# A two-layer decoder trunk on one core: the input also loaded with features on partitions, and a new order of the first loads and products

## The chip, the cores and the metric

The kernel runs on one NeuronCore of a Trainium2 chip. The metric is the device time of one execution in microseconds (us); lower is better. The engines are TensorE (PE in the profile; its weight loads are PEld), VectorE (DVE), ScalarE (ACT), GpSimd (POOL) and SyncE (SP), which here only issues DMAs.

## What is computed

The input `x` is 256 tokens of 1024 features in float32. Each of two layers computes, in the reference:

```
h = _rms_norm(x, attn_norm[layer])
x = x + _hybrid_mixer(h, w_in[layer], ...)
h = _rms_norm(x, ffn_norm[layer])
x = x + _swiglu(h, w_ffn_up[layer], w_ffn_down[layer])
```

with `_rms_norm(x, gain) = x * rsqrt(mean(x*x) + 1e-6) * gain`. The mixer begins with `proj = h @ w_in`, and goes on with four token mixers, gates, and the branch and output products. Only the very first of these products, `h @ w_in` of layer 0 with its norm, is touched by the change.

## The kernel before, in words

**Products in three parts.** Every float32 matrix is split in a high and a low part (`w_hi`, `w_lo`; `hT_hi`, `hT_lo`), rounded to TensorE's fp32r type. A product is three matmuls: high by high, high by low weight, low by high weight. ScalarE makes the high parts by a copy (L718 for weights, L722 for the left side), VectorE the low parts by subtraction (L977, L984).

**Units.** All weights go through the core once. They are cut into 144 units a layer; a unit is two blocks of 128 rows (`k`) by 512 columns, 512 KB. SP loads a unit into `raw` (six slots), ScalarE and VectorE split it into `w_hi` and `w_lo` (five slots), TensorE multiplies it with two token tiles `t` of 128 tokens: 2 k x 2 t x 3 parts = 12 matmuls of 512 columns. The first four units are the eight k blocks of the item `dq` of the first combined projection. ScalarE and VectorE work `AHEAD = 4` units ahead of TensorE; between units each engine takes other stages from a timetable by unit number, which the change leaves as it is.

**The norm.** The per-token factor of the norm is applied to products afterwards. The left side is `x * gain`, turned so that features lie on partitions: `hT[part][:, k, t*128:(t+1)*128]`. The squares for the factor are summed by `row_squares` (L734) on ScalarE.

**The first unit before.** SP issues the loads in written order: a half of a token tile of `x`, unit 0, a half tile, unit 1, two half tiles, units 2 to 5. ScalarE's queue loads the identity matrix and the norm's gains. TensorE runs 24 warm-up matmuls (L1674), turns the gains (L1680), turns `x` tile by tile with the identity (`turn_x`, L1655), with more warm-ups between, and VectorE multiplies the turned banks by the gain (`first_gain`, L1319). ScalarE and VectorE split the result, and TensorE starts the products of unit 0 (`first_products`, L1667). The unit 3 is the first that goes through the common routine `multiply` (L1636, L1637, L1640).

Signals are counting semaphores: `hi_ready` and `lo_ready` count split units, `unit_done` the units that TensorE has finished, `lhs_hi` and `lhs_lo` the parts of the left side.

Of the kernel before, what the change touches and what calls it, by code (L numbers as in the profile page):

```python
# [110 lines left out]
RING = 5  # L111
AHEAD = 4
# [196 lines left out]
def build(nc, x, attn_norm, ffn_norm, w_in, b_gate, w_branch, w_out, w_ffn_up, w_ffn_down, consts, params, out):  # L309
# [8 lines left out]
    with ExitStack() as ctx:  # L318
        def sb(name, shape, dt=F32, stack=ctx, align=32):
            return stack.enter_context(nc.sbuf_tensor(name, shape, dt, align_bytes=align))  # L320

        event_order = {}


        first_turn = {(*kind, t, b): 2 * b + t + 1 for kind in (("tr_norm", "attn"), ("norm", "attn"))
                      for t in range(TT) for b in range(2)}

        def signal(name, events):

            events = list(events)  # L330
            semaphore = ctx.enter_context(nc.semaphore(name))
            event_order[id(semaphore)] = {e: i + 1 for i, e in enumerate(events)}
            assert len(event_order[id(semaphore)]) == len(events)
            return semaphore

        def nth(semaphore, layer, event):

            order_in_layer = event_order[id(semaphore)]
            if layer == 0 and event in first_turn:
                return first_turn[event]  # L340
            return layer * len(order_in_layer) + order_in_layer[event]
# [27 lines left out]
        gain_rows = sb("gain_rows", [KD, P])  # L369
        gain_column = sb("gain_column", [P, KD])  # L370
# [56 lines left out]

        def hn(t):
            return wide[:, t, 0:D]
# [33 lines left out]
        stage_done = signal("stage_done", STAGE_EVENTS)  # L463
        lhs_hi = signal("lhs_hi", evac_events(ACT_ORDER))
        lhs_lo = signal("lhs_lo", evac_events(DVE_ORDER))
        warm_ready, bands_loaded = sem("warm_ready"), sem("bands_loaded")
        identity_loaded, consts_loaded, params_loaded = sem("identity_loaded"), sem("consts_loaded"), sem("params_loaded")
        x_loaded = [[sem(f"x_loaded{t}{j}") for j in range(2)] for t in range(TT)]
        gain_rows_loaded, gain_rows_turned = sem("gain_rows_loaded"), sem("gain_rows_turned")
        gain_column_ready = sem("gain_column_ready")  # L470
# [44 lines left out]
        hn_ready = {w: signal(f"hn_ready_{w}", [(t, j) for t in range(TT) for j in range(2)]) for w in ("attn", "ffn")}  # L515
# [26 lines left out]
        def _(sp):  # L542
# [21 lines left out]
            def load_x(t, j):  # L564
# [799 lines left out]
        def _(pe):  # L1364
# [324 lines left out]
            for t in range(TT):  # L1689
                turn_x(t, 1)  # L1690
# [81 lines left out]
```

## Time and profile before

| what | value |
| --- | --- |
| median of 3 runs | 866.67 us (866.63 to 866.77) |
| profiled execution, its own time | 866.5 us |
| its span, first to last instruction | 864.7 us |
| TensorE busy | 860.1 us (99% of the span), 4247 matmuls |
| VectorE busy | 599.4 us (69%) |
| ScalarE busy | 441.4 us (51%) |
| GpSimd busy | 110.1 us (13%) |
| DMA | 159.48 MB, mean 184 GB/s |

The span and the device time of the same execution differ by 1.8 us, which lies outside the first and last instruction. Busy times of different engines overlap. A matmul's own duration is its way through the array; the next one starts sooner, so the pace is read from the distance of starts. A group of n equal instructions in the timeline has one start and one length, from the first start to the last end.

### The profile page before, as it was taken

How to read it: one execution, taken by the hardware profiler on the slowest of the kernel's cores; microseconds unless marked ns; L12 is line 12 of the kernel's file. 1: busy time of each engine (PE TensorE's matmuls, PEld its weight loads, DVE VectorE, ACT ScalarE, POOL GpSimd, SP SyncE). 2: the span in 40 equal slices, each digit the busy share in tenths (PEclk: the TensorE clock that was granted, in tenths of full speed). 3: DMA queues.
4: the chain of work that ended last, by engine and by line, in shares of the span. 5: the costliest groups of instructions: out<-in, count | busy, mean ns of one | idle time of the engine just before them, and what ended most of it. 6: DMA issues, size and time to landing. Idle time of an engine off the chain costs nothing.

```text
span 864.7 us, 11127 instructions
## 1 busy us (share of the span) xinstructions
PE 860.1 (99%) x4247; PEld 712.1 (82%) x4247; DVE 599.4 (69%) x847; ACT 441.4 (51%) x639; POOL 110.1 (13%) x89
## 2 busy tenths in 40 slices
PE   9999999999999999999999999999999999999998
PEld 7888888888888888888888888888888888888886
DVE  5996887768777556654479868777597765565542
ACT  6556564754454444443375574556543644444431
POOL 0740100004501000000005401000064000000000
PEclk9999999999999999999999999999999999999999
DMA  9656565575657666555665455655666476665541
GB/s 331 201 185 179 173 189 171 161 236 183 207 171 237 192 178 190 192 175 193 171 184 166 130 183 168 194 176 175 210 195 193 127 238 177 190 185 181 194 146 50
DMA packets 87366, 159.48 MB, mean 184 GB/s; under 512 B 7432, under 2 KB 13712, under 8 KB 87312
## 3 DMA queue, kind: packets, MB, share of 16 engines
q1 hardware_dynamic: 87152, 158.69, 59.1%
q8 instruction: 34, 0.56, 0.2%
q14 instruction: 20, 0.16, 0.1%
q10 hardware_dynamic: 160, 0.07, 0.0%
HBM read 157.69 MB, written 1.05 MB: 184 GB/s over the span
## 4 chain that ended last, share of the span: by engine, by line
PE 99%; DMA 0%; DVE 0%; issue 0%
PE bulk L1636 30%; PE bulk L1640 30%; PE bulk L1637 30%; PE bankAB L1386 2%; PE bulk L1667 1%; PE bankAB L1577 1%; PE bankT L1530 0%; PE bankAB L1519 0%; DMA con<-consts_dram 0%; PE bankAB L1477 0%; PE bankAB L1395 0%; PE bankO L1490 0%; PE bankO L1548 0%; PE bankO L1577 0%; PE bankT L1577 0%; PE bankO L1395 0%
## 5 line engine op out<-in xcount | busy, mean ns | idle before, releaser
L977 DVE TENSOR_TENSOR w_lo<-raw,w_hi 128x1024 fp32r<-128x1024 f32 (+1 forms) x288 | 361.6, 1268 | 162.4 <-ACT w_hi L718 159.8
L718 ACT ACTIVATE w_hi<-raw 128x1024 fp32r<-128x1024 f32 (+1 forms) x288 | 299.0, 1048 | 237.5 <-PE bulk L1640 233.7
L1636 PE MATMUL bulk<-w_hi,hT_hi 128*128 128x512 f32 (+1 forms) x884 | 346.5, 392 | 0.0
L1637 PE MATMUL bulk<-w_lo,hT_hi 128*128 128x512 f32 (+1 forms) x884 | 340.8, 386 | 0.0
L1640 PE MATMUL bulk<-w_hi,hT_lo 128*128 128x512 f32 (+1 forms) x884 | 338.1, 386 | 0.0
L1640 PEld LDWEIGHTS bulk<-w_hi,hT_lo 128*128 128x128 f32 x884 | 165.7, 188 | 33.8
L1636 PEld LDWEIGHTS bulk<-w_hi,hT_hi 128*128 128x128 f32 x884 | 166.1, 188 | 33.3 <-issue 1.6
L1637 PEld LDWEIGHTS bulk<-w_lo,hT_hi 128*128 128x128 f32 x884 | 166.2, 188 | 31.4
L1636 PE MATMUL bulk<-w_hi,aT_hi 128*128 128x512 f32 x176 | 68.8, 391 | 0.0
L1640 PE MATMUL bulk<-w_hi,aT_lo 128*128 128x512 f32 x176 | 68.5, 389 | 0.0
L1637 PE MATMUL bulk<-w_lo,aT_hi 128*128 128x512 f32 x176 | 68.5, 389 | 0.0
L690 POOL TENSOR_TENSOR wide<-wide 128x512 f32<-128x512 f32 x24 | 46.1, 1943 | 125.2 <-DVE wide L1262 124.8
L656 POOL TENSOR_TENSOR wide<-wide,ropeA 128x512 f32<-128x512 f32 x8 | 12.0, 1494 | 210.9 <-DVE wide L1069 210.9
L1640 PEld LDWEIGHTS bulk<-w_hi,aT_lo 128*128 128x128 f32 x176 | 33.0, 188 | 7.0
L1637 PEld LDWEIGHTS bulk<-w_lo,aT_hi 128*128 128x128 f32 x176 | 33.0, 188 | 6.8
L1636 PEld LDWEIGHTS bulk<-w_hi,aT_hi 128*128 128x128 f32 x176 | 33.0, 188 | 6.7
L1636 PE MATMUL bulk<-w_hi,oT_hi 128*128 128x512 f32 x80 | 31.3, 391 | 0.0
L1640 PE MATMUL bulk<-w_hi,oT_lo 128*128 128x512 f32 x80 | 31.1, 389 | 0.0
L1637 PE MATMUL bulk<-w_lo,oT_hi 128*128 128x512 f32 x80 | 31.1, 389 | 0.0
L914 ACT ACTIVATE wide<-bulk,y_ffn 128x512 f32<-128x512 f32 (+1 forms) x24 | 14.4, 651 | 18.2 <-PE bulk L1640 16.0
L1252 DVE SCALAR_TENSOR_TENSOR wide<-bulk,y_attn,bias 128x512 f32<-128x512 f32 x32 | 22.5, 744 | 1.4 <-PE bulk L1640 1.4
L1276 DVE SCALAR_TENSOR_TENSOR wide<-bulk,y_ffn,wide 128x512 f32<-128x512 f32 (+1 forms) x24 | 15.9, 702 | 10.2 <-ACT wide L914 10.2
(259 smaller groups left out, 711.7 us busy)
## 6 DMA issues: line engine op xcount, KB each, us to landing
raw<-in_w_in_dram SPq DMA_DIRECT2D x112, 512.0 KB, 4.4
raw<-in_w_ffn_up_dram SPq DMA_DIRECT2D x80, 512.0 KB, 4.4
raw<-in_w_ffn_down_dram SPq DMA_DIRECT2D x44, 512.0 KB, 3.3
raw<-in_w_branch_dram SPq DMA_DIRECT2D x20, 512.0 KB, 4.1
raw<-in_w_out_dram SPq DMA_DIRECT2D x16, 512.0 KB, 3.3
bias<-in_b_gate_dram SPq DMA_DIRECT2D x16, 256.0 KB, 4.9
raw<-in_w_ffn_up_dram SPq DMA_DIRECT2D x16, 256.0 KB, 3.4
raw<-in_w_in_dram SPq DMA_DIRECT2D x8, 256.0 KB, 2.6
```

Of the source, the lines that this page charges most:

```text
L656: pool.tensor_tensor(ta, x, ropeA[:, i, t:t + 1, :].broadcast_to([P, 8, HD]), ALU.mult)
L690: ins = pool.tensor_tensor(m, m, wide[:, t, n * D + j * NC:n * D + (j + 1) * NC], ALU.add)
L718: act.activation(w_hi[:, g % RING, :, 0:width], raw[:, g % RAW, :, 0:width], ACT.Copy).then_inc(hi_ready, 1)
L914: act.activation(ff_tmp(t, p, width), item_bank(layer, ITEM_AT[item], t)[:, 0:width], ACT.Sigmoid, scale=y_ffn[:, t:t + 1]).then_inc(ff_si ...
L977: vec.tensor_tensor(w_lo[:, g % RING, :, 0:width], raw[:, g % RAW, :, 0:width], w_hi[:, g % RING, :, 0:width].bitcast(F32), ALU.subtract). ...
L1252: vec.scalar_tensor_tensor(out=wide[:, t, g * NC:(g + 1) * NC], in0=item_bank(layer, ITEM_AT[("gate", g)], t), scalar=y_attn[:, t:t + 1], ...
L1276: vec.scalar_tensor_tensor(out=s, in0=item_bank(layer, ITEM_AT[item], t)[:, 0:width], scalar=y_ffn[:, t:t + 1], in1=s, op0=ALU.mult, op1=A ...
L1386: ins = pe.matmul(dst, a[a_part], b[b_part], start=start and a_part + b_part == 0, stop=stop and a_part == 1, skip_group_check=True)
L1577: ins = pe.transpose(bank[name][:, k * P:(k + 1) * P], ff_act(t, p, blocks * P)[:, k * P:(k + 1) * P], identity)
L1636: pe.matmul(dst, hi, whi, start=(k == ks[0]), stop=False)
L1637: pe.matmul(dst, hi, wlo, start=False, stop=False)
L1640: ins = pe.matmul(dst, lo, whi, start=False, stop=(k == ks[-1]))
```

## The change

The host makes one more input, `turned_x`: the eight gain columns and `x` transposed, 128 partitions by 8 + 8 x 256 columns of float32, 1 MB. The plain `x` is still loaded, for the residual and the squares. The transposes of `x` and of the gains, the products with the gain on VectorE out of PSUM, the separate load of the identity and the load of the gains are gone. The gain is applied as the per-partition scale of ScalarE's copy and of VectorE's subtraction.

```diff
+WARM = 34
+FIRST_SQUARES = [1, 2]
...
+            def load_turned_x(e):
+                c0 = KD + e * 2 * SEQ
+                part = slice(c0 if e else 0, c0 + 2 * SEQ)
+                sp.dma_start(wide[:, 0, part], turned_x[:, part]).then_inc(turned_x_loaded[e], 16)
+            def load_x(t):
+                sp.dma_start(x_sb[:, t, :], x[0, t * P:(t + 1) * P, :]).then_inc(x_loaded[t], 16)
-            load_x(0, 0)
-            load_unit(0)
-            load_x(1, 0)
-            load_unit(1)
-            load_x(0, 1)
-            load_x(1, 1)
-            for g in range(2, RAW):
+            load_turned_x(0)
+            sp.dma_start(raw[:, 0, 1, :], w_in[0, P:2 * P, OFF["dq"]:OFF["dq"] + NC]).then_inc(raw_loaded[0], 16)
+            for g in range(1, 4):
+                load_turned_x(g)
                 load_unit(g)
+            load_x(0)
+            load_unit(4)
+            load_x(1)
+            load_unit(5)
...
+            def first_hi(k):
+                act.wait_ge(turned_x_loaded[k // 2], 16)
+                act.activation(hT[0][:, k, :], first_x[:, k, :], ACT.Copy, scale=first_gain[:, k:k + 1]).then_inc(lhs_hi, 1)
+            act.dma_start(raw[:, 0, 0, :], w_in[0, 0:P, OFF["dq"]:OFF["dq"] + NC]).then_inc(first_tile_loaded, 16)
+            act.preload_act_table_set("natural_log_exp_and_others")
+            first_hi(0)
+            first_hi(1)
+            act.wait_ge(first_tile_loaded, 16)
+            act.activation(w_hi[:, 0, 0, :], raw[:, 0, 0, :], ACT.Copy).then_inc(first_tile_ready, 1)
+            act.wait_ge(raw_loaded[0], loaded[0])
+            act.activation(w_hi[:, 0, 1, :], raw[:, 0, 1, :], ACT.Copy).then_inc(hi_ready, 1)
             for g in range(1, AHEAD):
+                first_hi(2 * g)
+                first_hi(2 * g + 1)
                 split_hi(g)
             for g in range(DEPTH * U):
+                if g in FIRST_SQUARES:
+                    row_squares(0, "attn", FIRST_SQUARES.index(g))
...
+            def first_lo(k):
+                vec.wait_ge(lhs_hi, k + 1)
+                vec.scalar_tensor_tensor(out=hT[1][:, k, :], in0=first_x[:, k, :], scalar=first_gain[:, k:k + 1],
+                                         in1=hT[0][:, k, :].bitcast(F32), op0=ALU.mult, op1=ALU.subtract).then_inc(lhs_lo, 1)
+            for g in range(AHEAD):
+                first_lo(2 * g)
+                first_lo(2 * g + 1)
                 split_lo(g)
...
+            def first_unit(u):
+                tiles = range(2 * u, 2 * u + 2)
+                for k in tiles:
+                    pe.wait_ge(lhs_hi, k + 1)
+                    if k == 0:
+                        pe.wait_ge(first_tile_ready, 1)
+                    else:
+                        pe.wait_ge(hi_ready, nth(hi_ready, 0, u))
+                    for t in range(TT):
+                        pe.matmul(item_bank(0, 0, t), hT[0][:, k, t * P:(t + 1) * P], w_hi[:, u, k % 2, :], start=(k == 0), stop=False)
+                for k in tiles:
+                    pe.wait_ge(lhs_lo, k + 1)
...
+                pe.wait_ge(lo_ready, nth(lo_ready, 0, u))
...
-            warm_up(24)
...
+            warm_up(WARM)
+            for u in range(KD // 2):
+                first_unit(u)
```

On TensorE the program's beginning before is this (`warm` is the warm-up operand, `con` holds the identity, `hT` is the left side):

```order
L1674 MATMUL bulk<-warm 128x128 x24
L1680 MATMUL bankO<-con,gain_rows 128x8
L1655 MATMUL bankAB<-con,x_sb 128x128 x4
L1674 MATMUL bulk<-warm 128x128 x8
L1655 MATMUL bankT<-con,x_sb 128x128 x4
L1674 MATMUL bulk<-warm 128x128 x6
L1667 MATMUL bulk<-w_hi,hT_hi 128x512 x2
L1667 MATMUL bulk<-w_hi,hT_lo 128x512 x2
L1667 MATMUL bulk<-w_hi,hT_hi 128x512 x2
L1655 MATMUL bankAB<-con,x_sb 128x128 x4
L1655 MATMUL bankO<-con,x_sb 128x128 x4
L1667 MATMUL bulk<-w_lo,hT_hi 128x512 x4
```

And this of the changed kernel, with the first two units:

```order
L1671 MATMUL bulk<-warm 128x128 x34
L1653 MATMUL bulk<-w_hi,hT_hi 128x512 x4
L1657 MATMUL bulk<-w_hi,hT_lo 128x512 x4
L1662 MATMUL bulk<-w_lo,hT_hi 128x512 x4
L1653 MATMUL bulk<-w_hi,hT_hi 128x512 x4
L1657 MATMUL bulk<-w_hi,hT_lo 128x512 x4
L1662 MATMUL bulk<-w_lo,hT_hi 128x512 x4
```

The 17 turning matmuls are gone, the warm-ups stand in one block of 34 instead of 24, 8 and 6, and every early unit is 4 + 4 + 4 products.

On SP, which issues the loads, the beginning before:

```order
L567 DMA x_sb<-in_x_dram 128x512
L556 DMA raw<-in_w_in_dram 128x2x512
L567 DMA x_sb<-in_x_dram 128x512
L556 DMA raw<-in_w_in_dram 128x2x512
L567 DMA x_sb<-in_x_dram 128x512 x2
L556 DMA raw<-in_w_in_dram 128x2x512 x6
L605 DMA con<-consts_dram 128x1028
```

and of the changed kernel (`wide` is a work area that holds the turned input at first):

```order
L571 DMA wide<-turned_x_dram 128x520
L578 DMA raw<-in_w_in_dram 128x512
L571 DMA wide<-turned_x_dram 128x512
L559 DMA raw<-in_w_in_dram 128x2x512
L571 DMA wide<-turned_x_dram 128x512
L559 DMA raw<-in_w_in_dram 128x2x512
L571 DMA wide<-turned_x_dram 128x512
L559 DMA raw<-in_w_in_dram 128x2x512
L575 DMA x_sb<-in_x_dram 128x1024
L559 DMA raw<-in_w_in_dram 128x2x512
L575 DMA x_sb<-in_x_dram 128x1024
L559 DMA raw<-in_w_in_dram 128x2x512 x3
```

A quarter of the turned input now stands ahead of each of the first four units, the token rows stand behind unit 3, and the first half of unit 0 has moved to ScalarE's queue.

ScalarE of the changed kernel begins so:

```order
L951 DMA raw<-in_w_in_dram 128x512
L952 ACT_TABLE_LOAD
L949 ACTIVATE hT_hi<-wide 128x256 x2
L956 ACTIVATE w_hi<-raw 128x512
L959 ACTIVATE w_hi<-raw 128x512
L949 ACTIVATE hT_hi<-wide 128x256 x2
L728 ACTIVATE w_hi<-raw 128x1024
L949 ACTIVATE hT_hi<-wide 128x256 x2
L728 ACTIVATE w_hi<-raw 128x1024
L949 ACTIVATE hT_hi<-wide 128x256 x2
L728 ACTIVATE w_hi<-raw 128x1024 x2
L744 ACTIVATE wide,ssq<-x_sb 128x512 x2
```

Unit 0 is split in two copies, the first of which TensorE can already use; the squares (L744) stand behind the split of unit 4, where before they stood behind that of unit 3.

## Rows read from the trace of the kernel before

**Rows 1.** Page, part 4: the chain that ended last, by engine.
```profile
PE 99%; DMA 0%; DVE 0%; issue 0%
```

**Rows 2.** Timeline of PE from 0 us: start, us, engine, line, instruction.
```profile
0.97 2.74 PE L1674 MATMUL bulk<-warm 128*128 128x128 bf16 x24 [0.97 <-DVE warm L1311]
4.15 0.27 PE L1680 MATMUL bankO<-con,gain_rows 8*128 8x8 f32 x1 [0.43 <-DMA con<-consts_dram]
6.34 1.11 PE L1655 MATMUL bankT<-con,x_sb 128*128 128x128 f32 x4
16.66 1.08 PE L1667 MATMUL bulk<-w_lo,hT_hi 128*128 128x512 f32 x4
17.58 0.39 PE L1636 MATMUL bulk<-w_hi,hT_hi 128*128 128x512 f32 x1
20.32 0.39 PE L1636 MATMUL bulk<-w_hi,hT_hi 128*128 128x512 f32 x1
```

**Rows 3.** Timeline of PE, narrow windows around the first products, one instruction each.
```profile
7.85 0.78 PE L1667 MATMUL bulk<-w_hi,hT_hi 128*128 128x512 f32 x1
8.43 0.55 PE L1667 MATMUL bulk<-w_hi,hT_hi 128*128 128x512 f32 x1
8.84 0.50 PE L1667 MATMUL bulk<-w_hi,hT_lo 128*128 128x512 f32 x1
9.17 0.39 PE L1667 MATMUL bulk<-w_hi,hT_lo 128*128 128x512 f32 x1
```

**Rows 4.** Window 4.2 to 8.9: engines' busy us, then PEclk, DMA share, GB/s.
```profile
4.20:8.90 4.70, 4.67 (x26) 3.76 (x26) 2.27 (x5) 2.31 (x4) 0.00 (x0) 1.00 1.01 354
```

**Rows 5.** Timeline of ACT and DVE: a whole unit, and 256-column operations.
```profile
5.31 1.06 ACT L718 ACTIVATE w_hi<-raw 128x1024 fp32r<-128x1024 f32 x1 [2.23 <-DMA raw<-in_w_in_dram]
8.70 1.22 DVE L977 TENSOR_TENSOR w_lo<-raw,w_hi 128x1024 fp32r<-128x1024 f32 x1
...
34.74 0.38 ACT L812 ACTIVATE keys_hi<-bankT 128x256 fp32r<-128x256 f32 x1 [0.51 <-PE bankT L1423]
35.02 0.38 ACT L813 ACTIVATE keys_hi<-bankT 128x256 fp32r<-128x256 f32 x1
...
43.24 0.41 DVE L1174 TENSOR_TENSOR keys_lo<-bankT,keys_hi 128x256 fp32r<-128x256 f32 x1
```

**Rows 6.** Timeline of SP's queue: start and us of the first issues.
```profile
0.72 0.38 SPq L567 DMA_DIRECT2D x_sb<-in_x_dram  x1
1.16 0.42 SPq L556 DMA_DIRECT2D raw<-in_w_in_dram  x1
1.63 0.46 SPq L567 DMA_DIRECT2D x_sb<-in_x_dram  x1
2.13 0.43 SPq L556 DMA_DIRECT2D raw<-in_w_in_dram  x1
3.60 8.46 SPq L556 DMA_DIRECT2D raw<-in_w_in_dram  x6
```

**Rows 7.** DMAs issued at 0.72, 1.16, 1.63, 2.13, 3.60: us to landing last.
```profile
x_sb<-in_x_dram SPq DMA_DIRECT2D x1, 256.0 KB, 3.2
raw<-in_w_in_dram SPq DMA_DIRECT2D x1, 512.0 KB, 4.1
x_sb<-in_x_dram SPq DMA_DIRECT2D x1, 256.0 KB, 4.7
raw<-in_w_in_dram SPq DMA_DIRECT2D x1, 512.0 KB, 6.1
raw<-in_w_in_dram SPq DMA_DIRECT2D x1, 512.0 KB, 7.3
```

**Rows 8.** Timeline, ACT and POOL later in layer 0, with their waits.
```profile
26.02 1.06 ACT L718 ACTIVATE w_hi<-raw 128x1024 fp32r<-128x1024 f32 x1 [1.24 <-PE bulk L1640]
...
22.19 1.50 POOL L641 TENSOR_TENSOR ropeA<-con,parameters 128x128 f32<-128x128 f32 x1 [20.92 <-DMA parameters<-params_dram]
30.66 1.29 POOL L656 TENSOR_TENSOR wide<-wide,ropeA 128x512 f32<-128x512 f32 x1 [4.06 <-DVE wide L1069]
```

More of the change, by code:

```diff
@@ L306, in constant_blocks, with build @@
     return {n: np.ascontiguousarray(b, dtype=np.float32) for n, b in blocks.items()}
-def build(nc, x, attn_norm, ffn_norm, w_in, b_gate, w_branch, w_out, w_ffn_up, w_ffn_down, consts, params, out):
+def build(nc, x, attn_norm, ffn_norm, w_in, b_gate, w_branch, w_out, w_ffn_up, w_ffn_down, consts, params, turned_x, out):
     cblocks = constant_blocks()
@@ L320, in sb, with signal @@
             return stack.enter_context(nc.sbuf_tensor(name, shape, dt, align_bytes=align))
[L322 to L328, printed above, removed]
+        event_order, more_in_first = {}, {}
+        first_norm = {("norm", "attn", t, b): 4 * (b + 1) for t in range(TT) for b in range(2)}
+        def signal(name, events, more=0):
             events = list(events)
@@ L1644, in multiply @@
                     ins.then_inc(early_done, 1)
-            def turn_x(t, b):
-                name = "ABTO"[2 * t + b]
-                pe.wait_ge(x_loaded[t][b], 16)
-                if name == "O":
-                    pe.wait_ge(gain_column_ready, 1)
-                take(name, lhs_lo, 0, ("norm", "attn", t, b))
-                for k in range(4):
-                    ins = pe.transpose(bank[name][:, k * P:(k + 1) * P], x_sb[:, t, (4 * b + k) * P:(4 * b + k + 1) * P], identity)
-                ins.then_inc(stage_done, 1)
@@ L1658, in first_products @@
-            def first_products(u, t, a_part, b_part):
-                event = ("norm", "attn", t, (2 * u) // 4)
-                dst = item_bank(0, 0, t)
-                if a_part:
-                    wait_low(0, event)
-                else:
-                    wait_high(0, event)
-                for k in range(2 * u, 2 * u + 2):
-                    ins = pe.matmul(dst, hT[a_part][:, k, t * P:(t + 1) * P], (w_hi, w_lo)[b_part][:, u, k % 2, :],
-                                    start=(k == 0 and a_part + b_part == 0), stop=(k == KD - 1 and b_part == 1))
-                return ins
+            def first_unit(u):
[10 more added lines that the diff above has]
+                    pe.wait_ge(lhs_lo, k + 1)
+                    for t in range(TT):
+                        pe.matmul(item_bank(0, 0, t), hT[1][:, k, t * P:(t + 1) * P], w_hi[:, u, k % 2, :], start=False, stop=False)
+                pe.wait_ge(lo_ready, nth(lo_ready, 0, u))
+                last = u == KD // 2 - 1
+                for t in range(TT):
+                    for k in tiles:
+                        ins = pe.matmul(item_bank(0, 0, t), hT[0][:, k, t * P:(t + 1) * P], w_lo[:, u, k % 2, :], start=False,
+                                        stop=k == KD - 1)
+                    if last and t == 0:
+                        ins.then_inc(early_done, 1)
+                ins.then_inc(unit_done, 1)
```

110 lines of the change are left out of this document (27 added, 83 removed).

## The prediction

> **What bounds the kernel.** I read the chain that ended last first: 99% of it is TensorE [rows 1]. Then the timeline of TensorE: after its first matmul at 0.97 us it stands idle for data once, 0.43 us at 4.15, and never again [rows 2]. So the time is the time at which the weight stream gets going, plus a fixed amount of matmul work. I fix a milestone that both kernels have: the first matmul of unit 4, which is behind 48 products (4 units of 12). Before, unit 3 begins at 17.58 and unit 4 at 20.32, that is 2.74 us for 12 products, **0.228 us a product** [rows 2]. The first product starts at 7.85 [rows 3]. All that is behind unit 4 is the same list of matmuls in both kernels, so a shift of this milestone is a shift of the end, if nothing later comes too late.
>
> Two things lie in those first 20.32 us besides the products at their pace. First, 48 products at 0.228 are 10.94 us; from 7.85 to 20.32 there are 12.47. The other 1.5 us are turning of x (eight of the turning matmuls lie between products), and products at a slower pace. Second, that slower pace: the first four starts are 7.85, 8.43, 8.84 and 9.17, distances of 0.58, 0.41 and 0.33 us, not 0.228 [rows 3]. The 24 warm-ups of 128 columns take 2.74 us, 0.114 each [rows 2], and four times that is 0.456 for 512 columns, twice 0.228. TensorE thus works at about half its pace (1.2 instead of 2.4 GHz) until 8.9 us. The granted-clock column says 1.00 for 4.2 to 8.9 us [rows 4], which the distances contradict; I go by the distances. The Trainium skill ("TensorE: Matmul & The Clock Gate", the caveats of Part 1) warns that the recorded clock events of trn2 have been seen to be unreliable; the trace agrees with the warning. If the column were right, no early product would be slow, which is rival A's sum below.
>
> **When the first product can start after the change.** It needs a quarter of the turned x, the first half of unit 0, and three copies on ScalarE. The two loads are 260 and 256 KB on two queues, both issued at about 0.72, as the first load of x was. Landings before are issue plus the time to landing [rows 6, 7]: the first 256 KB at 3.9, unit 0 at 5.3 (with 64 KB of identity that makes 832 KB), the second 256 KB at 6.3 (1088), unit 1 at 8.2 (1600), unit 2 at 10.9 (2624, with the two other halves of x). If 516 KB landed as the first 256 did, 3.9 us is the lower bound; unit 0's 5.3 is the upper one. In between by bytes: 3.92 + (516 - 320)/512 x 1.34 = 4.4 us. I take 4.4, as the two queues share the engines. The Trainium skill ("DMA: Bandwidth & Descriptors", queues, rings and completion order) says that each DMA engine takes turns between queues, packet by packet; by that neither of the two loads is done early, and the lower bound of 3.9 is out. No row shows two large first loads on two queues.
>
> Then ScalarE: two copies of 256 columns follow each other in 0.28 us (34.74, 35.02), and a whole unit of 1024 takes 1.06 [rows 5]; half of that with a fixed part is about 0.63. So 4.4 + 0.05 + 0.28 + 0.28 + 0.63 + 0.05 = **5.7 us** for the first product, against 7.85. Bounds: 5.2 with the early landing, 6.5 with the late one.
>
> **What follows it.** Second half of unit 0: it lands by 772 KB at about 5.1, is copied by 6.3, and TensorE needs it after two slow products, at 6.6. VectorE's low parts of x take 0.41 each [rows 5] and are ready at about 5.6 and 6.0. Its low part of unit 0 takes 1.22 from 6.3, ready at 7.5, needed after eight products, at 5.7 + 8 x 0.43 = 9.1. Unit 1 with its turned x is complete at 1540 KB: 6.33 + 452/512 x 1.9 = 8.0 us, split high at 9.1. TensorE ends unit 0 at about 9.9, so 0.8 us of cover; if this cover is gone, each us costs a us. Unit 2 (2308 KB) lands at 10.0, is ready at 11.1, needed at 12.6. Unit 3 (3076 KB) at the 393 GB/s between units 1 and 2 lands at 12.1, ready at 13.1, needed at 15.3. ScalarE spends 0.28 + 0.28 + 1.06 = 1.6 us a unit and VectorE 0.41 + 0.41 + 1.22 = 2.0, both under TensorE's 2.74.
>
> **Sum.** 48 products at 0.228: 10.94. Slow ones: from 5.7 to 8.9 with 0.41 to 0.456 a product, about 0.43: 7.4 products, each 0.2 too long, 1.5 us. Milestone at 5.7 + 10.94 + 1.5 = 18.1; I add 0.1 for handovers between parts: 18.2 against 20.32, a gain of **2.1 us**. The start itself hardly matters: an earlier or later start by 1 us moves the milestone by only 0.55, since more or fewer slow products fit before 8.9.
>
> **What costs nothing, and its cover.** The turned input is 1 MB more, some 2.6 us of DMA at 393 GB/s, all ahead of unit 4. Unit 4 comes at 4100 KB, 14.7 us, ready at 15.8 and needed at 18.2; unit 5 at 5124 KB, 17.4, ready 18.5, needed 20.9. That is 2.4 us of cover. From then on the loads run faster than the 2.74 us a unit in which TensorE eats them (1.3 us a unit at 393 GB/s). The issues behind the new ones on SP's queue (0.45 us each, [rows 6]) are eight more by unit 5, instead of six; the landings by bytes are later than the issues, so they do not count. The consts and parameters queue behind these: parameters, which before arrived for GpSimd at 22.19, come some 1.3 us later, and GpSimd's table work behind them (4.4 us to 26.6) then ends at 27.9; VectorE's result, for which GpSimd waited 4.06 us until 30.66, comes at 28.6 now [rows 8]. Cover 0.7 us, and behind it the turned queries aren't needed for five more units. The squares of x (four, 1.3 us for two by the 0.63 a copy) move behind unit 4's and 5's splits, where ScalarE waits on TensorE anyway: it did so for 1.24 us at 26.02 [rows 8]. One table load of ScalarE is gone; ScalarE is ahead there, so it gives nothing. VectorE's four products with the gain were on the way to the first split and are in the start above.
>
> **Rivals.** (B is the forecast above.)
>
> A. *The pace is full from the first products on.* For: 34 warm-ups in one block, up to about 4.7 us, where before there were 24 up to 3.7. Against: before, four more stretches of work followed and the pace rose only at 8.9. Then unit 0 ends at 8.5 and unit 1 waits for its split at 9.1: 9.1 + 36 x 0.228 = 17.3, gain 3.0, **863.7 us**.
>
> C. *The pace rises later than 8.9.* Before, TensorE worked without a gap from 4.15 on and rose 4.75 us later. After the change there is a gap of a us before 5.7; 4.75 behind it is 10.4: 11 slow products, 5.7 + 10.94 + 2.2 + 0.1 = 18.9, gain 1.4, 865.3. With a rise at 12.3 it is 15.4 products, 19.8, gain 0.5, 866.2. The Trainium skill ("TensorE: Matmul & The Clock Gate", Part 1) lets an idle array fall back to half clock, which speaks for this one; no row before shows how a gap of 1 us works here. I take **865.5 us** for it.
>
> D. *Slower, by the same mechanism.* Each slow product costs 0.2, so the gain is gone with (20.32 - 16.7)/0.2 = 18 slow products, a rise at 13.5 us, and the kernel is slower by over 1.7 us with 27 of them, a rise at 17.2. If all 48 stay slow the milestone is at 26.3 and the time 6 us longer, **872 us**. Waits for loads would have to break the stream again and again for that; the covers above speak against it.
>
> E. *It changes nothing*, as some later stage is short of its data and sets the milestone back. Unit 5 would have to land at 21.8 instead of 17.4. Against: TensorE had no such wait at all [rows 1, 2]. **866.7 us**.
>
> **Numbers.** The profiled execution took 866.5 us, and the median of the runs is 866.67, so the difference is made there: 866.67 - 2.1 = **864.6 us**. Chances: B 0.45, A 0.25, C 0.20, D 0.06, E 0.04. 0.2% of the time, 1.7 us, is about what a measurement tells from no change. B lies between 864.3 and 865.1 by the bounds of the start (5.2 to 6.5), and counts as faster 9 times in 10, A always, C 1 in 5: 0.25 + 0.40 + 0.04 = 0.69. D is slower 2 in 3 times, 0.04, and 0.27 is left for the same. The range takes in A's 863.7 with some room for a first load that is early, and C down to a gain of 0.6: 863.4 to 866.1.
>
> **What would show it.** In the changed profile: first product at 5.7 us (5.2 to 6.5); the distances of the starts at 0.41 to 0.46 until about 8.9 and 0.228 after; the 37th product (unit 3) at 15.4, the first of unit 4 at 18.2; no idle TensorE after the first product; unit 4's first to last matmul of the kernel as long as before. A wait before unit 1 at about 8.5 means rival A. Slow distances beyond 10 us mean C or D. I am wrong as a whole if TensorE waits for a load behind unit 4, or if the first product isn't earlier than 6.9.

## The result and the profile after

| what | before | after |
| --- | --- | --- |
| median of 15 runs each | 866.61 us (866.25 to 866.97) | 868.62 us (867.18 to 868.92) |
| profiled execution, its span | 866.5, 864.7 us | 868.86, 867.1 us |
| TensorE busy | 860.1 us | 857.8 us |

The ratio of after to before is 1.0018, 95% interval 1.0011 to 1.0024: slower by some 0.2%, where 864.6 us was forecast. The runs of after lie at two levels, seven at 867.18 to 867.31 us and eight at 868.62 to 868.92; both are above every run of before, and the 1.5 us between them is part of what has to be explained.

The timeline of TensorE after the change, the same places as [rows 2] and then the first wait that the old kernel did not have:

```profile
0.97 3.81 PE L1671 MATMUL bulk<-warm 128*128 128x128 bf16 x34 [0.97 <-DVE warm L1326]
6.33 1.23 PE L1653 MATMUL bulk<-w_hi,hT_hi 128*128 128x512 f32 x4 [1.55 <-ACT w_hi L956]
7.40 1.09 PE L1657 MATMUL bulk<-w_hi,hT_lo 128*128 128x512 f32 x4
...
16.53 1.07 PE L1662 MATMUL bulk<-w_lo,hT_hi 128*128 128x512 f32 x4
17.43 0.39 PE L1632 MATMUL bulk<-w_hi,hT_hi 128*128 128x512 f32 x1
...
28.09 0.39 PE L1636 MATMUL bulk<-w_hi,hT_lo 128*128 128x512 f32 x1
32.08 0.47 PE L1632 MATMUL bulk<-w_hi,hT_hi 128*128 128x512 f32 x1 [3.60 <-DVE wide L1084]
```

The first product starts at 6.33 and unit 4 at 17.43 instead of 20.32: **2.89 us are won**. Then the last product of unit 7 starts at 28.09, and the first of unit 8 at 32.08, after 3.60 us in which TensorE stands. Before, the same two products are here:

```profile
30.98 0.39 PE L1640 MATMUL bulk<-w_hi,hT_lo 128*128 128x512 f32 x1
31.26 0.47 PE L1636 MATMUL bulk<-w_hi,hT_hi 128*128 128x512 f32 x1
```

Unit 8 starts 0.28 us behind its predecessor, and the timeline prints no wait. That is not slack: the PSUM bank (the memory in which TensorE adds up its products) that it needs came free just then, as VectorE's timeline of before shows (start, us, line), with unit 8's low part first, then the norm of `dq`, whose last operation reads the bank:

```profile
23.87 1.23 DVE L977 TENSOR_TENSOR w_lo<-raw,w_hi 128x1024 fp32r<-128x1024 f32 x1 [0.50 <-ACT w_hi L718]
25.01 0.28 DVE L1010 TENSOR_TENSOR stat<-ssq 128x2 f32<-128x2 f32 x1
...
29.82 1.29 DVE L1069 TENSOR_TENSOR wide<-bulk,stat 128x512 f32<-128x512 f32 x2
```

29.82 + 1.29 is 31.11, and TensorE, which would have been ready at 31.21 (30.98 + 0.23), starts at 31.26. Item `dk` (units 8 to 11) takes over the PSUM bank of item `dq` (units 0 to 3), and `multiply` makes TensorE wait for both token tiles' release by VectorE. After the change the same three rows, and ScalarE's high part of unit 8 ahead of them:

```profile
23.59 1.06 ACT L728 ACTIVATE w_hi<-raw 128x1024 fp32r<-128x1024 f32 x1 [1.58 <-DMA raw<-in_w_in_dram]
```
```profile
24.69 1.23 DVE L992 TENSOR_TENSOR w_lo<-raw,w_hi 128x1024 fp32r<-128x1024 f32 x1 [2.19 <-ACT w_hi L728]
25.83 0.42 DVE L1025 TENSOR_TENSOR stat<-ssq 128x2 f32<-128x2 f32 x1
...
30.65 1.29 DVE L1084 TENSOR_TENSOR wide<-bulk,stat 128x512 f32<-128x512 f32 x2
```

All is 0.8 us later, not 2.9 us earlier. VectorE stands 2.19 us for ScalarE, which stands 1.58 us for unit 8's load. The load explains only that part: had it been there, ScalarE would have begun unit 8 at 22.0, behind the work that it does with one idle stretch of 0.23 us from 14.35 on (the splits of units 4 to 7, four squares of `x`, two of `dq`), where before it began it at 22.78. So the 2.9 us were not there for VectorE in any case, but some 0.8. The DMA rows of unit 8 (issued before at 16.21, after at 12.23; the last number is us to landing), then of the first two loads after:

```profile
raw<-in_w_in_dram SPq DMA_DIRECT2D x1, 512.0 KB, 4.8
```
```profile
raw<-in_w_in_dram SPq DMA_DIRECT2D x1, 512.0 KB, 11.3
...
wide<-turned_x_dram SPq DMA_DIRECT2D x1, 260.0 KB, 4.0
raw<-in_w_in_dram ACTq DMA_DIRECT2D x1, 256.0 KB, 4.2
```

Unit 8 lands at 21.0 before and at 23.55 after. It is issued 4 us earlier, but stands behind 1 MB more, which is some 2.6 us at the prediction's 393 GB/s.

Behind the wait the pace is halved for a while. Windows of TensorE after: us, busy (matmul starts), granted clock, DMA share, GB/s.

```profile
31.00:32.00 1.00, 0.00 (x0) 1.00 0.05 20
32.00:33.00 1.00, 0.92 (x4) 0.85 0.00 0
33.00:36.00 3.00, 3.00 (x9) 0.50 0.11 18
36.00:40.00 4.00, 4.00 (x23) 0.99 0.80 245
```

A granted clock of 0.50 is the 1.2 GHz level. About 8 products start 0.43 instead of 0.23 us after each other, 1.6 us. **The whole sum**: -2.89 at unit 4, +3.71 between units 7 and 8 (from 28.09 to 32.08 is 3.99, before 0.28), +1.6 by the pace: +2.4 us, and the spans differ by 867.1 - 864.7 = 2.4. Without the 1.6 it would be 867.25, the lower level of the runs.

### The profile page after: what moved, and what is told of

Same layout as the page of the kernel before. It is cut to its first block, busy times and chain, and to the rows that moved or that the text cites. A ratio compares the mean times of both kernels' runs of the same rounds, so it can differ in the third digit from the quotient of the medians.

```text
span 867.1 us, 11091 instructions
## 1 busy us (share of the span) xinstructions
PE 857.8 (99%) x4226; PEld 710.1 (82%) x4226; DVE 597.7 (69%) x846; ACT 441.7 (51%) x643; POOL 108.8 (13%) x89
## 4 chain that ended last, share of the span: by engine, by line
PE 96%; DMA 2%; DVE 1%; ACT 0%; issue 0%; SPq 0%
PE bulk L1632 29%; PE bulk L1636 29%; PE bulk L1633 29%; DMA raw<-in_w_in_dram 2%; PE bankAB L1382 2%; PE bankAB L1573 1%; PE bankT L1526 0%; PE bankAB L1515 0%; DVE w_lo L992 0%; PE bankAB L1473 0%; PE bankAB L1391 0%; PE bankO L1486 0%; PE bankO L1544 0%; PE bankT L1573 0%; PE bankO L1573 0%; ACT w_hi L728 0%
## 5 line engine op out<-in xcount | busy, mean ns | idle before, releaser
L924 ACT ACTIVATE wide<-bulk,y_ffn 128x512 f32<-128x512 f32 (+1 forms) x24 | 14.4, 650 | 18.2 <-PE bulk L1636 16.0
L1291 DVE SCALAR_TENSOR_TENSOR wide<-bulk,y_ffn,wide 128x512 f32<-128x512 f32 (+1 forms) x24 | 15.8, 701 | 10.2 <-ACT wide L924 10.2
```

Of the source, the lines that this page charges most:

```text
L924: act.activation(ff_tmp(t, p, width), item_bank(layer, ITEM_AT[item], t)[:, 0:width], ACT.Sigmoid, scale=y_ffn[:, t:t + 1]).then_inc(ff_si ...
L1291: vec.scalar_tensor_tensor(out=s, in0=item_bank(layer, ITEM_AT[item], t)[:, 0:width], scalar=y_ffn[:, t:t + 1], in1=s, op0=ALU.mult, op1=A ...
```

## The experiments

Theory: unit 8's low part paces VectorE's norm of `dq`, and this releases the bank of unit 8; the load of unit 8 is late by the 1 MB. Rivals: the slower pace has another cause; the early products cost the time; the later VectorE stages would take the gain anyway. Times are medians of 11 runs each (fewer where said), beside the kernel before on the same chip (866.45 to 866.63).

**1. The constants behind unit 9.** In the changed kernel, SP issues the load of the constants behind unit 9 instead of unit 7:

```diff
-                        if u == 1:
+                        if u == 3:
                             sp.dma_start(con[:, 0:first_band], ...)
```

> The changed kernel with one load moved on SP's queue: the 578 KB of constants are issued behind unit 9 instead of behind unit 7. My theory: unit 8 starts on TensorE when VectorE has normed the item dq (its PSUM bank is needed again), and VectorE's norm stands in its order behind the low part of unit 8, so behind the landing of unit 8 (23.55 us). 578 KB less ahead of it is 1.45 us: unit 8 lands at about 22.1, the norm ends at 30.4 instead of 31.9, TensorE's wait shrinks from 3.6 to about 2.1 us, and the time is 1.4 to 1.6 us lower than the changed kernel's, 865.8 with a fast pace kept and 867.3 with the slow pace after the wait. Rival: the wait is due to the squares of x that stand later on ScalarE, or the slow pace alone costs the time; then this load moves nothing, 868.6 or 867.2.

**866.19 us** (865.83 to 867.68; nine runs up to 866.41, two near 867.5); ratio 0.9998 (0.999 to 1.0007). The profiled execution is one of the two slower. Its TensorE:

```profile
30.82 0.47 PE L1632 MATMUL bulk<-w_hi,hT_hi 128*128 128x512 f32 x1 [2.06 <-DVE wide L1084]
```

Unit 8 starts 1.26 us earlier and the wait is 2.06 instead of 3.60; the starts are at half pace from 32.4 to 35. 578 KB out of unit 8's way took 1.1 us off the lower level (867.25 to 866.2) and 1.2 off the upper; the 2.4 us between the medians also come from more runs at the lower level. So the load is on the path. The forecast of the wait, 2.1 us, was met, but for another reason: unit 8 was issued at 12.51 and landed 8.5 us later, at 21.0, not at 22.1, and ScalarE took it only at 22.19, without a wait, at the end of a gapless row of work that begins with unit 5:

```profile
17.15 1.06 ACT L728 ACTIVATE w_hi<-raw 128x1024 fp32r<-128x1024 f32 x1 [0.29 <-DMA raw<-in_w_in_dram]
...
22.19 1.05 ACT L728 ACTIVATE w_hi<-raw 128x1024 fp32r<-128x1024 f32 x1
```

The wait that is left here is therefore not unit 8's load any more, but ScalarE's own work behind unit 5's load, and VectorE's norm behind that.

**2. The extra MB alone, in the kernel before.** The token rows loaded a second time behind unit 5, waited for by ScalarE, used by nothing:

```diff
+            sp.dma_start(wide[:, :, 1024:2048], x[0].rearrange("(t p) d -> p t d", p=P)).then_inc(extra_loaded, 16)
...
+                if g == 6:
+                    act.wait_ge(extra_loaded, 16)
```

> The kernel before with 1 MB more to load, issued behind unit 5 (x once more, into a part of the work area that nobody reads then); it computes the same. It has the transposes, the old first products and the old places of the squares. My theory: the loads of units 6 to 8 come 2.6 us later, unit 8 at 23.6 instead of 21.0, which is 0.8 us later than ScalarE needs it; VectorE's norm and so unit 8 on TensorE (31.26) come 0.8 to 0.9 us later, 867.4 in all. Rival (the bytes are harmless, the order of squares or the early start is to blame): no change, 866.6.

**867.38 us** (867.13 to 867.65), ratio 1.0011 (1.0002 to 1.0019), with the wait at the same place:

```profile
32.34 0.47 PE L1640 MATMUL bulk<-w_hi,hT_hi 128*128 128x512 f32 x1 [1.04 <-DVE wide L1073]
```

One MB ahead of unit 8 costs the old kernel 0.9 us by itself: it had no slack there. This one idle stretch of 1.04 us had no half pace behind it (the next starts are 32.65, 32.89). Right.

**3 and 4. The wait filled with warm-up products**, 60 and then 30, into a bank that is free there, so that the pace holds but the wait stays (changed kernel):

```diff
+                        for _ in range(30):
+                            pe.matmul(bank["A"][:, 0:P], warm[:, :], warm[:, :], start=True, stop=True)
```

> The changed kernel with 60 warm-up matmuls of 128 columns (into a PSUM bank that is free there) on TensorE between units 7 and 8, inside its wait of 3.6 us; at full pace they take 3.4 us. My theory: the two levels of the changed kernel's times (867.2 and 868.8) are one wait of the same length, after which TensorE's pace is in some executions half for 3 us and in others not. With the wait filled the pace stays, unit 8 starts at 32.1 as in the changed kernel and all runs lie at 867.2, within 0.2. Rival: the two levels come from something else, as loads that land at two different times; then both levels stay.

> The changed kernel with 30 warm-up matmuls between units 7 and 8, 1.7 us at full pace, which fit into the wait of unit 8 also where the first products were slow (60 did not: unit 8 came at 33.1). My theory of the two levels: an execution whose early products are fast waits 3.6 us at unit 8 and then works at half pace for 3 us, +1.6 us; one whose early products are slow waits under 2 us and keeps its pace. With 1.7 us of the wait filled the longest idle stretch is 1.9 us, and all runs lie at 867.2. Rival: the level comes from elsewhere, and a part of the runs stays at 868.8.

60: 867.35 us (867.13 to 869.66), seven runs up to 867.37 and four from 868.39 on; the forecast of one level was missed. In its profile (868.39 us) the first products were slow, TensorE came to the place later, and the 60 ran on to 33.3, past the release of the bank. 30: **867.25 us** (867.17 to 867.32, all 11):

```profile
29.92 1.85 PE L1682 MATMUL bankAB<-warm 128*128 128x128 bf16 x30
32.03 0.47 PE L1632 MATMUL bulk<-w_hi,hT_hi 128*128 128x512 f32 x1 [0.26 <-DVE wide L1084]
```

The upper level is gone and the lower one stays. So the upper level is the half pace behind an idle TensorE, and the lower one the late bank. This profile also shows what an early TensorE is worth here: it was done with unit 7 1.6 us later than in the changed kernel (its last product at 29.69, not 28.09), and unit 8 starts at the same time, 32.03 and 32.08.

**5. 24 warm-ups instead of 34** (`WARM = 24`, changed kernel), for the early pace.

> The changed kernel with 24 instead of 34 warm-up matmuls ahead of the first product. My theory: they set the pace of the first products (in the changed kernel these had full pace from 6.6 us on), but not the time: with 24 the first products may be slow until about 8.9 and unit 4 comes up to 1 us later than 17.4, and unit 8 still starts at 32.1, so the time is that of the changed kernel, 867.2 to 868.8. Rival: the early pace is part of the total, and the time rises by the 1 us.

867.21 us (865.9 to 868.9; 1.0007, 0.9998 to 1.0015), three runs at 865.9 to 866.2, seven at 867.2, one at 868.9. The profiled execution, at 866.22, has the first four products in 2.05 us, half pace, and no wait at unit 8; its VectorE did unit 8's low part at 23.39, not 24.69:

```profile
6.40 2.05 PE L1653 MATMUL bulk<-w_hi,hT_hi 128*128 128x512 f32 x4 [2.69 <-ACT w_hi L956]
```

The three fast runs were not forecast. In the profiled one, unit 8's load, issued at 12.37 behind the same loads, landed 9.9 us later, at 22.3 instead of 23.5; why, is open. So the bank came free sooner, and TensorE, with its slow beginning, came at 31.16 and had no wait. That a slower beginning costs nothing where the bank is late is shown by 4, and the seven runs here at 867.2 fit it; this profile mixes two things. The early pace is not a matter of the warm-ups alone: with 34 of them it is fast in the profiles of after and of 1, slow in 3, and in 4 fast for four products and then slow for eight.

**6. The bank released by a copy.** On top of 1, ScalarE copies `dq` out of the bank right behind its squares, and VectorE's norm reads the copy.

```diff
-                "dq": (normed, ("dq", t)), ...
+                "dq": (squares, ("dq", t)), ...
...
+                    if which == "dq":
+                        act.activation(xn("dq", t), item_bank(layer, ITEM_AT["dq"], t), ACT.Copy)
```

> The kernel with the constants loaded behind unit 9, and in both layers ScalarE copies the item dq out of its PSUM bank when it squares it (two copies of 512 columns more a layer); VectorE's norm reads the copy, and TensorE's unit 8 waits for ScalarE's squares instead of the norm. My theory: the bank is free at about 23 us and unit 8 starts right behind unit 7 at 28.4 where the start was fast; but VectorE still does its norm of 7 us before the low part of unit 9, which is ready at about 33.5 and wanted at 31.4, so a wait of about 2 us moves to unit 9. Time 865.5 to 866.0, a gain of 0.3 to 0.8 on the constants alone (865.8 to 866.4). Rival (the bank of dq is all that holds the start back): the whole 2.9 us of the start come through, 863.7.

**866.99 us** (866.74 to 867.38), where 865.5 to 866.0 was expected. The wait at unit 8 is gone, and the time was not won: I expected the next wait at unit 9. The chain of waits on TensorE shows where it is:

```profile
PE bulk L1634 <- DVE w_lo L994: 0.8, 1, 0.8
PE bankT L1421 <- ACT wide L817: 0.6, 1, 0.6
```

(line waiting, releaser, us in all, times, longest.) The first stands at unit 12, the second at the turning of `ss`. A missed expectation; it says that VectorE is late at the next stages too. The copy adds to that: ScalarE's two copies stand ahead of unit 8's split, which begins at 23.06 instead of 22.19 in experiment 1, and VectorE's low part of unit 8 at 24.17 instead of 23.28. All that VectorE does next is as much later, and this one is 0.8 us slower than experiment 1.

**7 to 14. The stages moved to give VectorE room.** Three forms of the timetable, each on the changed kernel with 1 and 6, and the same copy and timetable alone on the kernel before: "roomy" (norm of `dq` at slot 7, `ss` at 11, turning of `dq` at 15), "best" (norm at 6, the five casts of masks and sums on ScalarE), "best3" (norm at 7, `dk` copied out as well, `ss` at 12); w48 is with 48 warm-ups. For example:

```diff
-    (5, "qk_norm", "dq"), (7, "lambda_sums"), (9, "ss_evac"), ...
+    (7, "qk_norm", "dq"), (7, "lambda_sums"), (11, "ss_evac"), ...
```

> As copy, and VectorE norms dq behind the low part of unit 10 instead of unit 8 (slot 7 for 5), TensorE turns the item ss in slot 11 for 9 and the queries in slot 15 for 14. My theory: low parts of units 9 and 10 are ready at 26 and 28, the norm runs from 28 to 35, the low part of unit 11 is ready at 36.1 and wanted at 36.9, the turned ss at 36.3 and wanted at 36.6; TensorE has no wait behind its first product, and the start's 2.9 us come through: 863.7, within 0.5 (the early pace decides between 863.5 and 865). Rival: the DMA or VectorE bounds layer 0 somewhere else, and no order of stages helps: 866 or more.

> The kernel before (its old start, transposes on TensorE, no turned input) with the same bank copy and slots as roomy. My theory: it had just no wait at unit 8, so more room gives it nothing: 866.4 to 866.6 as before. Roomy against this one is then the worth of the new start by itself, 2.9 us. Rival: the slots themselves gain, and this one is faster than before too, by over 1 us.

> As roomy, but VectorE norms dq in slot 6 (behind the low part of unit 9), and the five 128x128 copies of masks and sums stand on ScalarE in slot 8, where it waits for the norm anyway, instead of on VectorE. My theory after roomy and copy: VectorE's own work between unit 8 and unit 12 (norm 7 us, masks and sums 3 to 4 us, low parts) is the next bound. Without the masks its work from 23 us to the low part of unit 12 is about 15 us, done at 38 to 39, and TensorE wants unit 12 at 40.2 where the start was fast. The tightest place is then the low part of unit 10, ready at 34.9 and wanted at 34.1. So the start's gain comes through but for 0.8 us: 864.4, and up to 865.2 where the early products are slow. Rival (the loads bound all of this stretch): 866 or more.

> As best, with 48 instead of 34 warm-ups, so that TensorE has no idle stretch between them and the first product (34 end at 4.8, the first product is at 6.3; 48 end at about 6.2). My theory: the early pace differs from execution to execution because of this idle stretch, and with it filled the first products are nearer to full pace in every run: the times are closer together than those of best, and their median is the same or up to 1 us lower. Rival: the idle stretch has nothing to do with the early pace; then the spread is as in best.

> The kernel before with its old start, and with the same copy of dq, slots and casts as best. My theory: the old start brings unit 8 at 31.3, VectorE's work is in time for it, and the time is that of before, 866.3 to 866.6. The difference between best and this one is what the new start is worth where VectorE has room, about 2 us. Rival: the slots and casts gain by themselves, and this one is at 865.5 or under.

> As best, with VectorE's norm of dq in slot 7 (behind the low part of unit 10), the item dk copied out of its bank by ScalarE too, and the turn of ss in slot 12. In best the gain of 0.9 us that TensorE still had at unit 14 (47.8 against 48.7) was gone at the next bank that waits for a norm, dk's (a wait of 0.5 at unit 16), and an execution with fast early products waited 2.3 us for the low part of unit 10. My theory: these were the two places left. With both gone the start comes through: 864.5 to 865.3 where the early products are slow, 863.7 to 864.5 where they are fast. Rival: VectorE's work up to about 60 us fills its time whatever the order, and the time stays at 866.3 to 867.

> As best3 with 48 warm-ups, by which the early products had full pace (four in 1.23 us from 6.51) and the runs of best_w48 lay 1.4 us above those of best. My theory: with room behind it the faster start is no longer paid back by a longer wait, and this one is the same as or faster than best3, 863.7 to 864.5. Rival (VectorE is full): it is at 866.5 or more again, as every us of earlier work becomes a us of waiting, and over 2 us of that cost the pace.

> The kernel before with its old start and the slots and copies of best3. My theory: it has no use for the room, 866.3 to 866.9, so that best3 against it shows the worth of the new start, 1.5 to 2.5 us. Rival: no difference between the two.

| | us | ratio | TensorE's waits in the profile |
| --- | --- | --- | --- |
| roomy | 870.38 (5 runs) | 1.0044 (1.0032 to 1.0057) | 3.2 at unit 12, then half pace |
| roomy on before | 867.83 | 1.0015 (1.0006 to 1.0024) | 0.8 at unit 12 |
| best | 866.86 | 1.0004 (0.9996 to 1.0013) | 0.3, 0.5, 0.3 |
| best, w48 | 868.24 | 1.0017 (1.0008 to 1.0026) | 2.3 at unit 10, then half pace |
| best on before | 866.88 | 1.0005 (0.9996 to 1.0013) | none |
| best3 | 868.93 (8 runs) | 1.0027 (1.0017 to 1.0037) | 1.6 in three, 1.4 |
| best3, w48 | 868.96 (8 runs) | 1.0027 (1.0016 to 1.0037) | 2.7 in three, 1.4 |
| best3 on before | 867.84 | 1.0015 (1.0006 to 1.0023) | 0.6 in two |

None beats before; all forecasts of a gain are misses. The old kernel with the same stages was forecast to lose nothing, and lost 1.3, 0.4 and 1.2 us (only the 0.4 lies within its interval of no change), so roomy and best3 cost time by themselves. Best and best on before were to differ by 2 us and are equal, 866.86 and 866.88: there the new start is worth nothing. And 48 warm-ups, from which the same or up to 1 us less was expected, made best 1.4 us slower. The rows for best3 are the plainest, the wait only moved from unit 8 to the low parts behind it and to the keys of the scores:

```profile
PE bulk L1635 <- DVE w_lo L1000: 1.6, 3, 0.9
PE bankAB L1385 <- DVE keys_lo L1197: 1.4, 1, 1.4
```

The window that I should have asked of the kernel before, VectorE's busy time by stage (the last two columns are DMA share and GB/s):

```profile
8.00:20.00 12.00, 10.78 (x13) 1.00 1.03 381
20.00:28.00 8.00, 6.32 (x13) 1.00 1.03 374
28.00:60.00 32.00, 30.19 (x56) 1.00 0.56 178
60.00:120.00 60.00, 47.71 (x88) 1.00 0.59 177
```

From 28 to 60 us VectorE is busy 30.19 of 32 us, 94%, where the page gives 69% over the whole. There is a second close fit in it: the low part of unit 12 starts at 41.77 and takes 1.21 us (its row stands in the last section), so it is ready at 42.98, and TensorE begins unit 12 at 43.16.

**15 to 18. The bank awaited for each token tile by itself**, just ahead of that tile's first product, on top of 1; with 16, 6 and no warm-ups at unit 8, and alone on the kernel before:

```diff
-                if high and k0 == ks[0] and layer * NITEM + n >= 2:
...
-                    for t in tiles:
...
-                        pe.wait_ge(sig, nth(sig, before, event))
+                fresh_bank = high and k0 == ks[0] and layer * NITEM + n >= 2
...
+                        if fresh_bank and i == 0:
...
+                            pe.wait_ge(sig, nth(sig, before, released))
```

> The kernel with the constants issued behind unit 9, with two edits for its wait at unit 8: the PSUM bank is awaited for each token tile by itself, just ahead of that tile's first product, and 16 warm-up products fill part of what is left. The norm of dq takes one operation of 1.29 us per token tile, so the first tile's half is free 1.3 us ahead of the second's. Theory (TensorE stands for the bank, and an idle TensorE there costs the pace behind it): unit 8's low parts are still needed by the first product, so the start moves forward by 1.3 us at most and probably by 0.6; the rest of the idle time is filled, no half pace follows, 865.2 to 865.6 us in all runs. Rival: the time won at unit 8 is returned at the next place where TensorE stands for VectorE, as in the kernels with moved slots: 865.9 us or more, with a wait at unit 10 to 12.

> The kernel before with the wait for the PSUM bank taken for each token tile by itself, and nothing else. It had 0.05 us of wait at unit 8 only. Theory: nothing to win there, 866.4 to 866.7 us. Rival: later turns of banks also win by it, and it is faster by 0.3 us or more; then that much of what tile_wait shows isn't due to the earlier start.

> The kernel with the constants behind unit 9 and the bank awaited for each token tile by itself, without warm-up products at unit 8. In the profile with 16 of them these themselves lay in the way: they ran from 29.85 to 30.73 us while the first tile's half was free at about 29.9. Theory (the wait at unit 8 is what costs): with a full pace early, unit 7 ends at 28.8, unit 8 starts at about 29.9, 0.9 us earlier than with both tiles awaited, idle for 1.1 us, and 1.04 us of idle time had no slow pace behind it: 865.3 to 865.9 us in such runs; with half pace early, TensorE arrives at 29.9 and does not wait, 866.0. No run above 866.6. Rival (VectorE paces what follows): the start at unit 8 moves but not the end, 865.9 to 866.4, and the profile shows the difference as a wait at a later stage.

> The same with 6 warm-up products of 0.057 us each, which take 0.34 us and so lie inside the wait if it is 1.1 us. Theory and rival as for the kernel without them; with an early full pace the same time as that one, with an early half pace 0.3 us more.

16 warm-ups: 866.05 us (865.87 to 866.45), ratio 0.9994 (0.9985 to 1.0003). Six: 866.14 (865.69 to 866.56), 0.9994 (0.9985 to 1.0003). None: 866.24 (865.89 to 866.44), 0.9995 (0.9986 to 1.0004). On before: 866.59 (866.47 to 866.73), 1.0. So no run is at the upper levels any more, and the medians are 0.4 to 0.5 us under before, which the ratios' intervals don't tell from nothing. The forecast for 16, 865.2 to 865.6 in all runs, was missed; of those for none, the rival's 865.9 to 866.4 came. The old kernel by itself gained nothing, as forecast. All three profiles of the changed form fell on executions with slow first products, so that the start at 29.9 was not seen. The one without warm-ups:

```profile
29.86 0.39 PE L1635 MATMUL bulk<-w_hi,hT_lo 128*128 128x512 f32 x1
30.50 0.47 PE L1631 MATMUL bulk<-w_hi,hT_hi 128*128 128x512 f32 x1 [0.25 <-DVE wide L1084]
```
```profile
PE bulk L1631 <- DVE w_lo L992: 0.3, 1, 0.3
PE bulk L1631 <- DVE wide L1084: 0.3, 1, 0.3
```

Unit 8 starts 0.76 us before its old 31.26. The other wait, for a low part, stands at unit 12. TensorE's row for it, then VectorE's:

```profile
42.87 0.50 PE L1631 MATMUL bulk<-w_hi,hT_hi 128*128 128x512 f32 x1 [0.30 <-DVE w_lo L992]
```
```profile
41.60 1.21 DVE L992 TENSOR_TENSOR w_lo<-raw,w_hi 128x1024 fp32r<-128x1024 f32 x1
```

The low part of unit 12 is ready at 42.81, only 0.17 us before its old 42.98, and of the 0.76 us at unit 8 there are 0.29 left at unit 12 (42.87 against 43.16). The rival had it: what is won at unit 8 is asked of VectorE by unit 12. The span of this execution is 864.5 us against 864.7.

## Why the prediction was wrong

**The step that failed** is in the paragraph on what costs nothing: the 1 MB was given a cover of 2.4 us at units 4 and 5, and "from then on the loads run faster" than TensorE eats them. True of the loads of units 4 to 7, for which TensorE never waited. But what TensorE needs at unit 8 is not the unit, it is a PSUM bank, and this comes 7.2 us after unit 8's low part *starts* (24.69 to 31.94), since VectorE's norm of `dq` stands behind it in VectorE's order. I followed each load to its split and to its product, and never followed what stands behind the split on the same engine. The squares of `x` were put at nothing in the same way, "where ScalarE waits on TensorE anyway", by a wait read at 26.02. They stand at 15.32 to 19.1, and from 14.35 to 22.0 ScalarE has 0.23 us of idle time. The sentence that all this leaves without ground is the first one on the sum: a shift of unit 4 is a shift of the end "if nothing later comes too late". In rival E I wrote "TensorE had no such wait at all [rows 1, 2]" and read that as slack. It was an exact fit, 31.11 against 31.21. The line of the text that would have decided, "I am wrong as a whole if TensorE waits for a load behind unit 4", is what happened, through two engines. E had the form right, a later stage that sets the start back, and was given 0.04; it named data where it was a bank, and its 866.7 was too low.

**The price of it.** Between units 7 and 8 the kernel gives back 3.7 us where 2.9 had been won. That the load's place is a part of this is shown by 1 and 2: 578 KB less ahead of unit 8 starts it 1.26 us earlier, 1 MB more costs the old kernel 0.9 us. That the rest is ScalarE's row of work up to 22.0 is read from the rows of after and of 1; no run took a piece of this work away. The other 1.6 us, half pace behind the idle stretch, is rival D's mechanism in small, 8 slow products, shown by 4, in which it is gone. D asked for waits that "break the stream again and again"; one was enough.

**The first product** came at 6.33, not 5.7, inside the bounds 5.2 to 6.5. The loads landed at 4.7 and 4.9 (taken: 4.4), and ScalarE's two copies of 256 columns took 0.91 and not 0.56:

```profile
4.76 0.91 ACT L949 ACTIVATE hT_hi<-wide 128x256 fp32r<-128x256 f32 x2 [2.33 <-DMA wide<-turned_x_dram]
5.58 0.61 ACT L956 ACTIVATE w_hi<-raw 128x512 fp32r<-128x512 f32 x1
```

**The early pace.** The profiled run has four products in 1.23 us [rows 3 gave 0.58, 0.41 and 0.33 a start]: rival A, with unit 4 at 17.43 where A had 17.3. Other profiles with the same 34 warm-ups have 2.05 us for the four, and there the pace rises at about 10.2 us, not at 8.9; the one without warm-ups at unit 8 (tile_only) goes on so:

```profile
8.28 1.91 PE L1656 MATMUL bulk<-w_hi,hT_lo 128*128 128x512 f32 x4
...
11.02 1.09 PE L1652 MATMUL bulk<-w_hi,hT_hi 128*128 128x512 f32 x4
```

Their unit 4 comes at 18.9 to 19.2, which is rival C's 18.9. So A and C are seen, and B's 18.2, the forecast, in no profile. In the changed kernel neither matters: with a bank at a fixed time, an earlier TensorE only waits longer, and can lose its pace behind the wait.

**The rest.** "No idle TensorE after the first product" holds up to unit 8 only. Unit 1 did not wait, where A expected it to. The milestone gained 2.89 us for the 2.1 forecast in this execution, and 1.1 to 1.5 in those with a slow start, so the 2.1 lies between two values and is neither. GpSimd's work on the parameters began 2.5 us later, not 1.3 (24.70 against the 22.19 of [rows 8]), and TensorE never stood for it.

**Could the gain be kept?** Not by what I tried. Experiment 1 with the wait per tile (15, 17, 18) is the best of them, 866.05 to 866.24 us against 866.6, under what the intervals tell. The copy and the moved stages return the time behind unit 8, up to the scores, nearly always in a wait for VectorE. That VectorE's work from unit 8 to the scores bounds the start of this kernel is supported by these waits and by the window above; no run made this work shorter, and which of its operations could be taken away altogether was not tried.

## What to carry to other kernels

An engine that never waits can still have no slack: before counting an earlier start as won, look for every hand-over of a buffer or bank on the bounding engine, and compare the time of the release with the time of the need, also where no wait is printed. Follow a delayed load past its first user to all that stands behind that user in the same queue. An earlier start counts only if every engine of the chain to the next hand-over is earlier too: here ScalarE could be 0.8 us earlier, not 2.9. And ask for the busy share of the second engine in the stretch concerned, not over the whole span.

## What the runs showed of the hardware

The pace of the first products differs between executions with the same beginning, 1.23 or 2.05 us for four, behind the same 34 warm-ups; what decides it is open. The granted clock of the column is 1.00 from 7 to 8 us in both after and tile_only, though six products start in that window in the one and four in the other.

The granted clock fell to 0.50 behind idle stretches of 3.60 us (after), 3.21 (roomy), 2.30 (best, w48), 2.06 (experiment 1) and 1.84 (30 warm-ups, ahead of the first product: 0.50 from 8 to 11 us), and not behind one of 1.04 (experiment 2). Nor did it behind 2.07 us in best3, w48, of which these are TensorE's row and the window behind it (window, us, busy us and starts, granted clock, DMA share, GB/s):

```profile
38.91 0.50 PE L1635 MATMUL bulk<-w_hi,hT_hi 128*128 128x512 f32 x1 [2.07 <-DVE w_lo L1000]
```
```profile
39.00:41.00 2.00, 2.00 (x9) 1.00 0.51 129
```

So the length of the idle stretch alone does not decide it, and these runs do not show what else does.

The load of unit 8 landed at two times with the same loads ahead of it: at 23.5 in after, and at 22.3 in the profile of experiment 5, whose kernel differs in the number of warm-ups only.

The same VectorE operation has several lengths. In the kernel before, the low part of a unit takes 1.22 us [rows 5]; 2.00 us at 36.97, while GpSimd works at 36.55 and at 37.85; and 1.21 again at 41.77, when GpSimd has just ended. VectorE's timeline, then GpSimd's:

```profile
36.97 2.00 DVE L977 TENSOR_TENSOR w_lo<-raw,w_hi 128x1024 fp32r<-128x1024 f32 x1
...
41.77 1.21 DVE L977 TENSOR_TENSOR w_lo<-raw,w_hi 128x1024 fp32r<-128x1024 f32 x1
```
```profile
36.55 1.35 POOL L656 TENSOR_TENSOR wide<-wide,ropeA 128x512 f32<-128x512 f32 x1
37.85 1.72 POOL L657 TENSOR_TENSOR wide<-wide,ropeB 128x256 f32<-128x256 f32 x1
...
40.34 1.29 POOL L663 TENSOR_TENSOR wide<-wide 128x512 f32<-128x512 f32 x1
```

The Trainium skill ("SBUF — State Buffer", "SBUF: two separate sides") has VectorE and GpSimd share one pair of ports, which an operation of VectorE with two inputs in SBUF and one of GpSimd that reads SBUF cannot use together. The trace agrees with it here, in that the operation is 0.8 us longer beside GpSimd's and not behind them; no run took GpSimd's work away, so the cause stays argued. It would make VectorE's tight stretch from 28 to 60 us tighter by GpSimd's rotations in it.
